# A two-layer block with eight routed experts: expert weight tiles loaded in pairs, 2 MB a transfer

## The reference

```python
def swiglu(h, w_gate, w_up, w_down):
    return (jax.nn.silu(h @ w_gate) * (h @ w_up)) @ w_down

def moe_swiglu(h, w_router, w_gate, w_up, w_down):
    logits = (h @ w_router).astype(jnp.float32)
    top_val, top_idx = lax.top_k(logits, 2)
    top_w = jax.nn.softmax(top_val, axis=-1)
    gates = jnp.sum(jax.nn.one_hot(top_idx, 8, dtype=jnp.float32) * top_w[..., None], axis=-2)
    out = jnp.zeros_like(h)
    for e in range(8):
        out = out + gates[..., e:e + 1] * swiglu(h, w_gate[e], w_up[e], w_down[e])
    return out
```

## Time and profile before

| what | value |
|---|---|
| median of 3 runs | 1967.89 us (1966.92 to 1968.2) |
| span of the profiled execution, first to last instruction | 1965.6 us |
| PE, DVE, ACT busy | 1944.0, 1193.1, 1050.1 us |
| mean granted TensorE clock | 0.998 |
| bytes read from HBM | 536.33 MB (10^6) |
| expert stage | some 440 to 1285 us |

### The profile page before, as it was taken

How to read it: one execution, slowest core, us unless ns; L and a number is a source line. 1 busy time by engine, 2 the same in 40 slices (tenths; PEclk the granted TensorE clock), 3 DMA queues, 4 the chain that set the end, 5 groups by cost and what they waited for, 6 DMA issues and landing times.

```text
span 1965.6 us, 26432 instructions
## 1 busy us (share of the span) xinstructions
PE 1944.0 (99%) x10046; PEld 1462.2 (74%) x10047; DVE 1193.1 (61%) x1896; ACT 1050.1 (53%) x1747; POOL 59.8 (3%) x86
## 2 busy tenths in 40 slices
PE   9999999999999999999999999999999999999998
PEld 7788888887667766676657776578777888878786
DVE  5665557675446545564448676166666876666775
ACT  6564446655345534564447555165556655456663
POOL 0000000014000000000000000000200000020000
PEclk9999999999999999999999999999999999999999
DMA  7346555368999999999999999945444355444443
GB/s 293 129 170 254 189 182 186 119 284 318 417 421 421 421 420 420 421 421 421 421 420 421 420 420 421 402 162 205 150 150 150 129 193 193 172 150 152 149 150 108
DMA packets 79191, 542.83 MB, mean 276 GB/s; under 512 B 10948, under 2 KB 11204, under 8 KB 14416
## 3 DMA queue, kind: packets, MB, share of 16 engines
q1 hardware_dynamic: 78240, 539.41, 69.7%
q0 software_dynamic: 672, 1.55, 0.2%
q10 hardware_dynamic: 144, 0.10, 0.0%
HBM read 536.33 MB, written 5.51 MB: 276 GB/s over the span
## 4 chain that ended last, share of the span: by engine, by line
PE 88%; DMA 6%; DVE 3%; ACT 2%; issue 1%; SPq 0%; ACTq 0%; DVEq 0%
PE bank L258 22%; PE bank L260 22%; PE bank L259 22%; PE bank L2175 8%; PE bank L820 4%; PE bank L2185 4%; DMA moe_ring<-in_moe_tiles 3%; DMA ring<-in_moe_tiles 1%; DVE w_low L236 1%; DVE w_low L233 1%; DMA ring<-in_hy_tiles 1%; PE bank L2090 1%; PE bank L3136 1%; ACT w_high L225 1%; PE bank L3158 0%
## 5 line engine op out<-in xcount | busy, mean ns | idle before, releaser
L258 PE MATMUL bank<-w_high,xT_high 128*128 128x512 f32 x1520 | 609.4, 401 | 2.8 <-DVE xT_low L535 1.4
L260 PE MATMUL bank<-w_high,xT_low 128*128 128x512 f32 x1520 | 593.8, 391 | 0.0
L259 PE MATMUL bank<-w_low,xT_high 128*128 128x512 f32 x1520 | 592.7, 390 | 0.0
L258 PEld LDWEIGHTS bank<-w_high,xT_high 128*128 128x128 f32 x1520 | 285.5, 188 | 81.1 <-issue 16.2
L260 PEld LDWEIGHTS bank<-w_high,xT_low 128*128 128x128 f32 x1520 | 285.3, 188 | 62.0
L259 PEld LDWEIGHTS bank<-w_low,xT_high 128*128 128x128 f32 x1520 | 286.0, 188 | 54.6
L233 DVE TENSOR_TENSOR w_low<-ring,w_high 128x1024 fp32r<-128x1024 f32 x170 | 209.9, 1235 | 188.8 <-ACT w_high L225 188.5
L225 ACT ACTIVATE w_high<-ring 128x1024 fp32r<-128x1024 f32 x170 | 179.8, 1058 | 182.9 <-PE bank L260 163.8
L236 DVE TENSOR_TENSOR w_low<-ring,w_high 128x1024 fp32r<-128x1024 f32 x170 | 209.2, 1230 | 0.0
L233 DVE TENSOR_TENSOR w_low<-moe_ring,w_high 128x1024 fp32r<-128x1024 f32 x105 | 128.3, 1222 | 112.7 <-ACT w_high L225 112.0
L228 ACT ACTIVATE w_high<-ring 128x1024 fp32r<-128x1024 f32 x170 | 178.2, 1049 | 0.0
(11 more groups left out here) (421 smaller groups left out, 2534.9 us busy)
## 6 DMA issues: line engine op xcount, KB each, us to landing
moe_ring<-in_moe_tiles SPq DMA_DIRECT2D x212, 1024.0 KB, 18.2
ring<-in_hy_tiles SPq DMA_DIRECT2D x103, 1024.0 KB, 4.7
ring_wide<-in_moe_tiles SPq DMA_DIRECT2D x61, 1024.0 KB, 17.7
ring<-in_moe_tiles SPq DMA_DIRECT2D x60, 1024.0 KB, 18.2
ring<-in_ffn_tiles SPq DMA_DIRECT2D x17, 1024.0 KB, 4.8
ring_wide<-in_ffn_tiles SPq DMA_DIRECT2D x16, 1024.0 KB, 4.7
ring_wide<-in_gla_in_tiles SPq DMA_DIRECT2D x6, 1024.0 KB, 9.8
ring<-in_sb_in_tiles SPq DMA_DIRECT2D x6, 1024.0 KB, 4.7
```

The costliest lines, as they stand in the source:

```text
L258: nc.tensor.matmul(out, x[0], w[0], start=start, stop=False, **more)
L259: nc.tensor.matmul(out, x[0], w[1], start=False, stop=False, **more)
L260: return nc.tensor.matmul(out, x[1], w[0], start=False, stop=stop, **more)
```

## The change

Tiles 42 to 319 are transferred in pairs. In DRAM the tiles of an expert are stored two by two, 16 KB a partition: guA with guB of a step, dn of an even step with dn of the next step of the same expert. A pair is one DMA of 2 MB into two neighbouring places of one tensor (`TOGETHER`: 9 and 10, 0 and 1, 2 and 3, 4 and 5, 6 and 7); both tiles signal through the first place's semaphore. SP waits for the previous tiles of both places. A pair stands in the order where its first tile stood, so the second down tile comes ahead of the tiles between the two. Tiles whose mate has gone already, or that are outside 42 to 319, come singly, as half of the 16 KB row. By the new list 138 of 201 transfers are pairs. Place 8 belongs to no pair: it holds no tile between 36 and 320.

```diff
+TOGETHER = ((RING_WIDE + 5, RING_WIDE + 6), (0, 1), (2, 3), (4, 5), (6, 7))
+PAIRED = range(42, 320)
...
+def tile_place(kind, c):
+    c = c % MOE_STEPS
+    return (MOE_STEPS + c // 2, c % 2) if kind == "dn" else (c, int(kind == "guB"))
...
 def expert_tile(K, expert, kind, c):
-    n = 3 * (c % MOE_STEPS) + ("guA", "guB", "dn").index(kind)
+    n, half = tile_place(kind, c)
+    return K.I["moe_tiles"][bass.ds(expert, 1), n, :, half * SLOT:(half + 1) * SLOT].rearrange("e p n -> (e p) n")
+def expert_tiles(K, expert, kind, c):
+    n, half = tile_place(kind, c)
+    assert half == 0
     return K.I["moe_tiles"][bass.ds(expert, 1), n].rearrange("e p n -> (e p) n")
...
+    def mate(u):
+        kind, (q, c) = step_of(u)
+        if kind == "guA":
+            return u + 1
+        return u // PER * PER + number["dn", rounds[u // PER].at[q, c + 1]] if kind == "dn" and c % 2 == 0 else None
+    transfers, begun = [], set()
+    for u in early + [u for u in range(N_TILES) if u not in early]:
+        if u in begun:
+            continue
+        other = mate(u) if u in PAIRED else None
+        transfers.append((u,) if other is None or other in begun else (u, other))
+        begun.update(transfers[-1])
...
+        usable = [slot for slot in CYCLE if v < LAST or slot >= SPLIT]
+        if len(tiles) == 2:
+            places = min((p for p in TOGETHER if set(p) <= set(usable)), key=lambda p: max(free_at(last_in[slot]) for slot in p))
...
+        def both(slot):
+            tensor, at = (K.ring, slot) if slot < RING else (K.wide, slot - RING) if slot < RING_WIDE else (extra, slot - RING_WIDE)
+            return tensor[:, at:at + 2, :].rearrange("p i n -> p (i n)")
...
+                def load(tiles, src):
+                    memory, name, _ = runs[tiles[0]]
+                    for u in tiles:
+                        if previous[u] is None:
+                            continue
+                        n, v = divmod(previous[u], PER)
+                        if narrow_tile(n, v):
+                            sync.wait_ge(W.used, first + n * PER + v + 1)
+                        else:
+                            sync.wait_ge(W.split, made_splits[n, v])
+                    sync.dma_start(both(slot_at(tiles[0])) if len(tiles) == 2 else memory, src).then_inc(W.landing[name], 16)
...
+    arrays["moe_tiles"] = np.stack([np.stack([np.concatenate([tiles_of["guA", c], tiles_of["guB", c]], 1) for c in range(MOE_STEPS)]
+                                             + [np.concatenate([tiles_of["dn", c], tiles_of["dn", c + 1]], 1) for c in range(0, MOE_STEPS, 2)]) for tiles_of in experts])
```

More of the change, by code:

```diff
@@ L1932, in moe, with step_of @@
     early = [u for u in range(PER) if not narrow_at(u)][:EARLY]
-    transfers = early + [u for u in range(PAIRS * PER + SPLIT) if u not in early]
-    done, slot_of, previous = [0.0], [None] * len(transfers), [None] * len(transfers)
-    for u in range(len(transfers)):
+    N_TILES = PAIRS * PER + SPLIT
+    def step_of(u):
+        kind, s = order[u % PER]
+        return kind, rounds[u // PER].seq[s]
+    def mate(u):
[3 more added lines that the diff above has]
+        return u // PER * PER + number["dn", rounds[u // PER].at[q, c + 1]] if kind == "dn" and c % 2 == 0 else None
@@ L1939, in moe @@
-    for v, u in enumerate(transfers):
-        if v <= MOE_RING:
-            slot = (CYCLE + (ONCE,))[v]
+    last_in, before = {}, set()
+    for tiles in transfers:
+        v = len(before)
+        usable = [slot for slot in CYCLE if v < LAST or slot >= SPLIT]
+        if len(tiles) == 2:
+            places = min((p for p in TOGETHER if set(p) <= set(usable)), key=lambda p: max(free_at(last_in[slot]) for slot in p))
+        elif v <= MOE_RING:
+            places = ((CYCLE + (ONCE,))[v],)
@@ L1942, in moe @@
         elif v < PAIRS * PER:
-            slot = min((slot for slot in CYCLE if v < LAST or slot >= SPLIT), key=lambda slot: free_at(last_in[slot]))
+            places = (min(usable, key=lambda slot: free_at(last_in[slot])),)
         else:
[L1945 to L1948, removed]
+            places = (v - PAIRS * PER,)
@@ L1950, in moe @@
+        for u, slot in zip(tiles, places):
+            slot_of[u], previous[u] = slot, last_in.get(slot)
+            assert previous[u] is None or (previous[u] < u and all(w in before for w in range(previous[u] + 1)))
+        last_in.update(zip(places, tiles))
+        before.update(tiles)
     slot_at = lambda u: slot_of[u]
@@ L2527, in _ @@
                     placed_expert = [0 if m == 1 else sync.value_load(table[0:1, E + 1 + m:E + 2 + m], min_val=0, max_val=E - 1) for m in range(2 * pair, 2 * pair + 2)]
-                    for v in range(pair * PER if pair else EARLY, (pair + 1) * PER):
-                        u = transfers[v] - pair * PER
-                        load(pair, u, expert_tile(K, placed_expert[rounds[pair].place(pair, rounds[pair].seq[order[u][1]][0]) - 2 * pair], order[u][0], rounds[pair].seq[order[u][1]][1]))
+                    for v, tiles in enumerate(transfers):
+                        if tiles[0] // PER != pair or v < EARLY:
+                            continue
+                        u = tiles[0] % PER
+                        kind, (q, c) = step_of(tiles[0])
+                        load(tiles, (expert_tiles if len(tiles) == 2 else expert_tile)(K, placed_expert[rounds[pair].place(pair, q) - 2 * pair], kind, c))
                         if v == NORM_AT:
@@ L2543, in _ @@
                 for u in range(SPLIT):
-                    load(PAIRS, u, next_tile(K, u))
+                    load((PAIRS * PER + u,), next_tile(K, u))
                 overflows["SP"] = overflowing(K, sync, table)
@@ L2634, in moe_overflow @@
     landed, per_slot = [], {}
-    for i, (kind, c) in enumerate(order):
+    for i in range(PER):
         name = run0[i][1]
```

20 lines of the change are left out of this document (10 added, 10 removed).

## The result

The changed kernel takes **1984.97 us** (median of 4, 1984.08 to 1986.36) against 1967.41 for the kernel before on the same chip: +17.6 us, ratio 1.0095, 95% interval 1.0083 to 1.0107. The forecast was +6.4 us and its range ended at 1981.5. The sign was right, the size was not.

The account below looks back on a forecast made before the run. DMA engines and PE were taken as both at their limit in the expert stage. New waits 12.2 us less 4.5 old gave +7.7, less 1.2 to 1.3 at the end: +6.4, so 1974.3 us; range 1967.5 to 1981.5.

Parts of the forecast that it names:

- the ladder: Rates at 2, 4 and 8 KB packets (382, 407, 421 GB/s), extended to 16 KB: 611.9 ns, 428 GB/s.
- walk: Calculation over the new transfers and places with PE's measured pace and three rules; +7.7 us at the last expert tile.
- packets gain nothing: Rival: 16 KB packets are cut in two or their fixed part grows; +12.2 us, 1980.1; chance 0.09.
- a third: Rival: loads' fixed part is only some 3.5 ns, 2.476 us per MB; +10.5, 1978.4; chance 0.06.
- step 1: Down pair 43 and 49: issued at 534.0, data from 536.2, engines still for 4.6 us, landing at 541.1.
- the faster rival: Ring has slack enough, queue never runs dry, PE's 4.5 us of waits vanish: -4.5, 1963.4; chance 0.09.
- The rival of lateness that is absorbed: ACT rounds up to three tiles ahead, so landings slip up to 3 us unseen: +2.5, 1970.4; chance 0.17.
- both places must be free: Expert stage: a pair's issue follows the later release of its two places by 0.2 us; walk +2.7 us.
- joined landings: Expert-stage pairs: both tiles have landed only at the end of the pair's transfer; walk +5.8 us.
- step 4: Later gaps: new waits of 0.6 us at tile 104, 2.6 and 0.7 at 145 and 146, 2.0 and 0.7 at 229 and 230.
- gaps of some 20 us against 12 won: Whole expert stage: the stream's gaps come to some 20 us, while longer packets win 12 us over 276 paired tiles.
- bound of 15 for the worst case: Upper corner of the sum: a start of 2.8 us together with no gain from packets, 15 us.

Follow-up runs that it names:

- The run pair: Changed kernel with pairs stacked so each 2 MB transfer has 8 KB packets, 1990.84 us, beside the changed kernel with 16 KB packets, 1984.97 us.
- runs at fixed depth: SP issues only after an earlier transfer has landed: kernel before, three in flight 1975.05 us, two 2032.1 us; changed kernel, two in flight 1994.13 us.
- both waits: Changed kernel with each pair as two 1 MB transfers, the waits for both places ahead of both: 1981.26 us.
- two in flight: Kernel before, from the 43rd to the 320th transfer each issued only when the transfer two before it has landed: 2032.1 us.
- one transfer of 8 KB packets: Changed kernel with the tiles of a pair one behind the other in memory, so a 2 MB transfer has 8 KB packets: 1990.84 us.
- own waits: Changed kernel with each pair as two 1 MB transfers, each waiting for its own place alone: 1969.95 us.
- gate/up pairs: Changed kernel with only gate/up tiles paired (92 transfers of 2 MB), down tiles single: 1966.13 us.
- the layout alone: Changed kernel's memory layout with no tile paired; order, places and waits of the kernel before: 1965.77 us.
- two of 1 MB with one landing: Changed kernel with each pair as two 1 MB transfers, both places waited for, both tiles taken only when both have landed: 1989.53 us.

## Why the prediction was wrong, and where it was right

*Right: the packets.* 611 ns and 428 GB/s, as worked out from the ladder. The run pair gives 6.6 us for it at the end (walk 5.1), with 3.4 us less at the lower clock in it. The rivals "packets gain nothing" and "a third" fall; by the records the stream won 9.7 us. The Trainium skill's three cycles per packet (DMA: Bandwidth & Descriptors, Why small descriptors are slow) come to an estimated 3.9 us for 276 tiles (276 x 0.014); the trace disagrees: 611 ns stand for two packets of 311 to 312, so 11 to 13 ns a packet saved, and 9.7 us.

*Right: the first gap.* (43, 49) was issued at 533.9 (534.0 forecast):

```profile
L2570 SPq DMA_DIRECT2D ring_wide<-in_moe_tiles x1: 339/339/339, 533.9 to 533.9; - x1
...
DMA to landing us min/median/max: 7.8/7.8/7.8
```

7.8 us to landing is 4.89 and a start of 2.9, where I took 2.2 and bounded at 2.8. That is step 1's miss, 0.7 us. With 2.8 everywhere the walk ends at +8.8, so in the walk's own terms it isn't the bulk.

*Right: the layout costs nothing* (its own run), and the condition of the faster rival, both places free by 529.4, was not met (issue at 533.9). The rival of lateness that is absorbed falls too: PE took on 16 us more of idle time. *Right, too: the tiles at which PE waits, and that little comes after 229.* The fixed 2.0 us per transfer that the prediction takes from the Trainium skill (DMA: Bandwidth & Descriptors, Anatomy of one DMA) stand there for transfers issued from GpSimd. Those here are issued from SP, so the figure is not for them.

*Wrong: the term "both places must be free".* The third rule of the walk failed: "data flow 2.2 us after it or when the queue before is done, and a pair takes 4.89 us". It took the queue for one server that is done when the transfer ahead has landed, and so a transfer issued 3 us ahead for as good as one issued 15 us ahead. The records show sixteen engines that are done at different times, and a start of 2.7 to 3.0 us for a pair: 18 transfers with leads of 2.2 to 5 us came 14.6 us late in sum, where the rule has nothing. Waiting for both places was priced at 2.7 us by the walk and measured 11.3. The price of joined landings, 5.8 and measured 8.6, was short in the same direction. In steps: 3.5 new us at tile 62 stood (3.6 from 53 to 62, the lateness of PE). Of step 4, 0.6 at 104 and 2.6 + 0.7 at 145 were 7.5 from 62 to 145, and 2.0 and 0.7 at 229 and 230 were 6.1. In these rounds come the (92, 93) to (100, 109) and (184, 193) transfers, with leads of 1.2 to 3.5 us and 1.2 to 1.8 us lost by each.

*Wrong: the clock had no term.* The prediction puts the cost of a wait at the wait, and says nothing of the granted clock. Of the 21.4 us at tile 335, 4.5 came from three stretches at the lower clock, 1.6 of them at tile 62, 1.3 at 145 and 1.6 at 229. Each stands beside a wait of over 3 us; that the waits are their cause is argued from this alone.

*Wrong: gaps of some 20 us against 12 won.* 31 more than before, and about 10 won. The bound of 15 for the worst case took the start and the packets as the only unknowns. That the engines run apart, and that a long wait lowers the clock, had no bound.

**What stays open.** Why the engines run apart is not settled. That instruction packets hold one engine up is shown by coincidence in time and by the runs at fixed depth; no run takes an instruction packet away. The single-engine starts above are an account after the fact, one start fitted to all: the 23 transfers of the changed kernel fit with 2.6 to 2.8 us, the 9 of both waits lost 18.0 us, which takes 2.4 to 2.5, and the 252 of the kernel before with two in flight 90.1, which takes 2.2 to 2.3. No run was forecast by this rule. The walk with the changed kernel's own losses by lead gives 14.4 for both waits and 25.6 for one transfer of 8 KB packets (+14.6 and +24.2 measured), but 7.8 for own waits and 3.1 for gate/up pairs (+3.3 and -0.2), so it is a description and no law. What a wait must be like to lower the clock is open too: before, 2.95 us of waiting at 1281.0 stand beside the lower clock, while 2.92 at 1280.2 with the layout alone, and 3.27 at 1304.0 with one transfer of 8 KB packets, do not.

## What to carry to other kernels

Joining transfers saved 11 ns per packet pair here and was paid for in queue depth, twice: the pair waits for the later of two places, and its first tile waits for the second. Join only tiles that are used one after the other and whose places come free together (the gate/up pairs here cost nothing; the down pairs, whose second tile is used three to nine tiles after the first, brought all of the +17.6 on top of them). When a plan thins a DMA queue, don't price it by the landings alone: look at the arrivals of the sixteen engines one by one, since those that are ahead run dry first. And price a wait of TensorE with the clock that follows it: three waits over 3 us cost 4.5 us more than their own length.

## What the runs showed that I had not expected

The median time to landing says little about a stream: own waits and both waits differ by 11 us of kernel time with medians of 12.5 to 13.1 and 11.5 to 12.9. Three transfers of 1 MB in flight, 7.4 us from issue to landing for 18.2, still carry the stream at 412 GB/s and cost 8 us in all; two carry 376:

```profile
500.00:1250.00 750.00, 737.98 (x3998) 501.60 (x3996) 420.73 (x504) 372.63 (x549) 6.09 (x6) 1.00 1.01 412
```

```profile
500.00:1250.00 750.00, 693.48 (x3673) 470.29 (x3669) 383.09 (x460) 341.21 (x502) 6.08 (x6) 0.98 0.95 376
```

(three, then two in flight; the profiled execution with two has a span of 2046.1, above its median of 2032.1). And a 2 MB transfer of 8 KB packets takes what two of 1 MB with one landing take, 1990.84 and 1989.53 us.
